# A three-stage fp32 block on one core: staged first transfers, a third load by rows of 128, and the last convolution taps ahead of a weight split

## The reference, cut to what matters

```python
h = rms_norm(x, mix_pre_g[0])                      # 256 x 2048
z = h @ ab_w_in                                    # 2048 x 3072 of weights
u_pool, v, gate = z[:, :1024], z[:, 1024:2048], z[:, 2048:]
c = causal_depthwise_conv(v * sigmoid(gate), conv_w) + conv_b    # 31 taps, 1024 channels
y_conv = silu(layer_norm(c, ln_g, ln_b))
m = concat(multiscale_pool(u_pool), y_conv) @ ab_w_out
x = x + rms_norm(m, mix_post_g[0])
...                                                # two MLPs, a short convolution, attention, gating
```

## Time and profile before

| what | value |
|---|---|
| median of 3 runs | 2687.98 us |
| the profiled execution's own time | 2690.7 us |
| its span | 2689.0 us |
| TensorE busy | 2679.8 us of the span (100%) |
| VectorE busy | 1872.4 us (70%) |
| ScalarE busy | 1292.8 us (48%) |
| GpSimd busy | 278.2 us (10%) |
| read from HBM | 511.47 MB, 191 GB/s over the span |

### The profile page before, as it was taken

How to read it: one execution, slowest core, us unless ns; L and a number is a source line. 1 busy time by engine, 2 the same in 40 slices (tenths; PEclk the granted TensorE clock), 3 DMA queues, 4 the chain that set the end, 5 groups by cost and what they waited for, 6 DMA issues and landing times.

```text
span 2689.0 us, 31099 instructions
## 1 busy us (share of the span) xinstructions
PE 2679.8 (100%) x12001; PEld 2218.5 (83%) x12001; DVE 1872.4 (70%) x2495; ACT 1292.8 (48%) x1635; POOL 278.2 (10%) x263
## 2 busy tenths in 40 slices
PE   9999999999999999999999999999999999999999
PEld 7888888888888888888888888888888888888887
DVE  6878777666866767776677676667767757765564
ACT  6765544434444454444544444344445446544452
POOL 4851100000000010000110000000011001000000
PEclk9999999999999999999999999999999999999999
DMA  7545665555555556555555555555555645455554
GB/s 248 183 169 180 215 211 183 184 202 188 193 192 195 194 183 213 193 197 194 187 188 204 203 188 186 190 188 203 188 188 179 211 173 182 169 200 194 188 188 156
DMA packets 267972, 515.58 MB, mean 192 GB/s; under 512 B 8450, under 2 KB 27956, under 8 KB 267316
## 3 DMA queue, kind: packets, MB, share of 16 engines
q1 hardware_dynamic: 267556, 513.34, 55.4%
q10 hardware_dynamic: 272, 0.26, 0.0%
HBM read 511.47 MB, written 2.10 MB: 191 GB/s over the span
## 4 chain that ended last, share of the span: by engine, by line
PE 98%; DMA 1%; DVE 1%; ACT 0%; issue 0%; SPq 0%
PE bank L786 32%; PE bank L788 32%; PE bank L787 32%; PE bank L837 1%; DMA x_res<-in_x 0%; DMA w_raw<-in_ab_w_in 0%; PE bank L854 0%; PE bank L1027 0%; DVE w_lo L765 0%; PE bank L988 0%; PE bank L1041 0%; PE bank L1014 0%; DVE w_lo L755 0%; DVE bank L1783 0%; PE bank L1048 0%
## 5 line engine op out<-in xcount | busy, mean ns | idle before, releaser
L765 DVE TENSOR_TENSOR w_lo<-w_raw,w_hi 128x1024 fp32r<-128x1024 f32 x952 | 1183.1, 1265 | 493.5 <-ACT w_hi L747 487.8
L747 ACT ACTIVATE w_hi<-w_raw 128x1024 fp32r<-128x1024 f32 x956 | 974.7, 1056 | 589.9 <-PE bank L788 432.9
L786 PE MATMUL bank<-w_hi,A_lo 128*128 128x512 f32 x2432 | 952.5, 392 | 2.3 <-DVE A_lo L1468 0.8
L788 PE MATMUL bank<-w_hi,A_hi 128*128 128x512 f32 x2432 | 947.2, 389 | 0.0
L787 PE MATMUL bank<-w_lo,A_hi 128*128 128x512 f32 x2432 | 946.7, 389 | 0.0
L786 PE MATMUL bank<-w_hi,B_lo 128*128 128x512 f32 x1408 | 548.7, 390 | 0.0
L788 PE MATMUL bank<-w_hi,B_hi 128*128 128x512 f32 x1408 | 547.9, 389 | 0.0
L787 PE MATMUL bank<-w_lo,B_hi 128*128 128x512 f32 x1408 | 547.8, 389 | 0.0
L786 PEld LDWEIGHTS bank<-w_hi,A_lo 128*128 128x128 f32 x2432 | 456.6, 188 | 98.4 <-DVE w_lo L765 2.3
L788 PEld LDWEIGHTS bank<-w_hi,A_hi 128*128 128x128 f32 x2432 | 456.4, 188 | 95.8
L787 PEld LDWEIGHTS bank<-w_lo,A_hi 128*128 128x128 f32 x2432 | 456.7, 188 | 93.2
(11 more groups left out here) (178 smaller groups left out, 975.7 us busy)
## 6 DMA issues: line engine op xcount, KB each, us to landing
w_raw<-in_ffn_w SPq DMA_DIRECT2D x256, 1024.0 KB, 5.1
w_raw<-in_w_in SPq DMA_DIRECT2D x88, 1024.0 KB, 4.9
w_raw<-in_sc_w_in SPq DMA_DIRECT2D x48, 1024.0 KB, 5.1
w_raw<-in_ab_w_out SPq DMA_DIRECT2D x16, 1024.0 KB, 5.0
w_raw<-in_sc_w_out SPq DMA_DIRECT2D x16, 1024.0 KB, 5.1
w_raw<-in_w_out SPq DMA_DIRECT2D x16, 1024.0 KB, 5.3
w_raw<-in_ab_w_in SPq DMA_DIRECT2D x28, 512.0 KB, 4.6
w_raw<-in_ab_w_in SPq DMA_DIRECT2D x8, 1024.0 KB, 5.1
```

The lines of the kernel that those rows point to most:

```text
L747: e.activation(w_hi[:, s % SPLIT_SLOTS, :], raw_step(s), ACT.Copy).then_inc(hi_made, 1)
L765: e.tensor_tensor(w_lo[:, slot, :], raw_step(s), w_hi[:, slot, :].bitcast(F32), ALU.subtract).then_inc(lo_made, 1)
L786: e.matmul(ps, lo[:, kt, tok], wh, start=first, stop=False)
L788: ins = e.matmul(ps, hi[:, kt, tok], wh, start=False, stop=last)
```

## The change

The first transfers are issued in stages: in front of most of them SyncE now waits until an earlier one has landed. Load 2 is brought by four `load_rows` of 256 KB in place of one `load_weights` with two pieces of 512 KB, and `BEGIN` covers 6 steps, so that steps 4 and 5 are split by 128-row parts too. ScalarE and VectorE make the halves of group 1 of `x` in two parts, with step 2's weights split between them and step 3's behind. VectorE does step 57's taps right behind step 56's, which puts them ahead of the low half of step 60.

```diff
-        BEGIN = 2 * STEPS_PER_LOAD
-        rows_loaded = [semaphore(f"rows_loaded{i}") for i in range(2 * GK)]
+        BEGIN = RAW_SLOTS * STEPS_PER_LOAD
+        rows_loaded = [semaphore(f"rows_loaded{i}") for i in range(RAW_SLOTS * GK)]
...
-            before = LOADED[n - RAW_SLOTS] if n >= RAW_SLOTS + 2 else 0
+            before = LOADED[n - RAW_SLOTS] if n >= 2 * RAW_SLOTS else 0
...
             load_rows(0, 0)
             load_rows(0, 1)
             e.dma_start(x[:, :, CH // 2:CH], x_dram[:, :, CH // 2:CH]).then_inc(x_loaded[0], 16)
+            e.wait_ge(x_begun, 16)
             load_rows(0, 2)
+            e.wait_ge(rows_loaded[0], 16)
             load_rows(0, 3)
+            e.wait_ge(rows_loaded[1], 16)
             load_x(1)
-            for k in range(GK):
-                load_rows(1, k)
+            e.wait_ge(x_loaded[0], 16)
+            load_rows(1, 0)
+            e.wait_ge(rows_loaded[2], 16)
+            load_rows(1, 1)
+            e.wait_ge(rows_loaded[3], 16)
+            load_rows(1, 2)
+            load_rows(1, 3)
+            e.wait_ge(x_loaded[1], 16)
             load_x(2)
-            load_weights(2)
+            e.wait_ge(rows_loaded[4], 16)
+            load_rows(2, 0)
+            e.wait_ge(rows_loaded[5], 16)
+            load_rows(2, 1)
+            e.wait_ge(rows_loaded[6], 16)
+            load_rows(2, 2)
+            load_rows(2, 3)
+            e.wait_ge(x_loaded[2], 16)
             load_x(3)
...
-            hi_x(0, 1)
+            for h in two:
+                hi_half(0, 1, h)
+                split_to(e, split_hi, at, STEPS_PER_LOAD + h)
...
-            lo_x(0, 1)
+            for h in two:
+                lo_half(0, 1, h)
+                split_to(e, split_lo, at, STEPS_PER_LOAD + h)
...
-                for tap in taps_at(DVE_TAPS, POS[c, i], DVE_TAP_TO):
-                    dve_tap(e, *tap)
+                s = POS[c, i]
+                for step in (s, s + 1) if s == DVE_TAP_TO - 2 else (s,) if s < DVE_TAP_TO - 1 else ():
+                    for tap in taps_at(DVE_TAPS, step, DVE_TAP_TO):
+                        dve_tap(e, *tap)
```

More of the change, by code:

```diff
@@ L1084, in hi_scaled, with hi_half @@
                 e.activation(halves[buf][0][:, kt + 1, :], view[:, 1, :], ACT.Copy, scale=gains[1]).then_inc(hi_cast(*key), 1)
+            def hi_half(p, g, h):
+                kt = GK * g + 2 * h
+                hi_scaled("A", kt, [par_col(PRE_COL[p], kt + k) for k in two], "pre", p, g, h)
             def hi_x(p, g):
                 for h in two:
-                    kt = GK * g + 2 * h
-                    hi_scaled("A", kt, [par_col(PRE_COL[p], kt + k) for k in two], "pre", p, g, h)
+                    hi_half(p, g, h)
             def hi_tile(p, g, tt):
@@ L1470, in lo_scaled, with lo_half @@
                 ins.then_inc(lo_cast(*key), 1)
+            def lo_half(p, g, h):
+                kt = GK * g + 2 * h
+                lo_scaled("A", kt, [par_col(PRE_COL[p], kt + k) for k in two], "pre", p, g, h)
             def lo_x(p, g):
                 for h in two:
-                    kt = GK * g + 2 * h
-                    lo_scaled("A", kt, [par_col(PRE_COL[p], kt + k) for k in two], "pre", p, g, h)
+                    lo_half(p, g, h)
             def lo_part(p, g, tt, h):
```

## The result

The changed kernel is slower: 2695.7 us, the median of 9 runs (2693.97 to 2697.49), against 2687.98 us before (9 runs, 2687.55 to 2688.68). The ratio is 1.0028, 95% interval 1.0018 to 1.0038. I had forecast 2687.6 us, no change. A loss of more than 0.2% had a chance of 0.05, 0.04 of it in the last of my rivals, the slow stages at 2696.4 us. The time lies outside the range of 2684.6 to 2690.6 us.

A forecast was written before the change was run, and what follows sets the result against it. TensorE bounds the kernel, busy 2679.8 of 2689.0 us. Start 0 and taps -0.4 us, put to the median of 2687.98 us, gave 2687.6 us; range 2684.6 to 2690.6 us, about 0.85.

The forecast's parts named there:

- the slow stages: Rival, start: waits leave transfer engines empty, 512 KB still takes 8.8 us, step 6 at 40.7 us: 2696.4 us; chance 0.04.
- The bound: TensorE's waits: only some 3.5 us, 0.13% of the time, could be won.
- The path to load 3: SyncE's queue: groups 1 to 3 in stages of 4.4 us, small transfers, then load 3, landing at 27.5 us.
- my bad end of 31.5 us: Load 3's latest believed landing, with 5.5 us per 512 KB transfer; step 6 then at 35.9 us.
- Load 3 lands later: Rival, start: 5 us a stage and 8 us for load 3, step 6 at 34.2 us: 2689.9 us; chance 0.15.
- The estimate of 3.2 us for 512 KB: Staged transfers: the skill page's figures give 3.2 us for 512 KB; step 6 would start at 29.5 us.
- The same difference put to it gives 2687.98 - 0.4: Final sum: the median lies 2.7 us below the profiled execution; the same difference gives 2687.6 us.
- my forecast of 31.9 us: Start: load 3 lands at 27.5 us and step 6 starts at 31.9 us, as in the profile before; sum 0.
- The clock: Rival, wait before step 6: clock falls to 1.2 GHz, costing 1.9 us: 2689.5 us; chance 0.16.
- Gain 0.33 to 0.5 us: Taps near 190.8 us: moved early, they remove TensorE's wait of 0.33 us; 0.4 us taken.
- Load 2 by rows and the order of group 1: Start: VectorE's extra 0.8 us is covered, step 4 can begin 0.45 us sooner; the order adds no instruction.

The follow-up runs named there:

- experiment 5: The kernel before, unchanged, profiled once more: own time 2687.83 us, span 2686.1 us.
- experiment 1: The changed kernel without its eleven waits on SyncE's queue: 2687.88 us, ratio 1.0002 to the kernel before.
- experiment 6: The kernel before with the early taps alone: 2688.08 us, ratio 1.0000.
- experiments 9: The changed kernel itself, timed and profiled a second time: 2694.49 us, ratio 1.0024 to the kernel before.
- experiment 2: The kernel before with the eleven waits alone, load 2 still two pieces of 512 KB: 2694.01 us, ratio 1.0020.
- Experiment 3: The changed kernel with 40 more transposes of the identity on TensorE ahead of step 6: 2693.73 us, ratio 1.0022 to the kernel before.
- Experiment 12: The changed kernel without waits, small transfers on GpSimd's queue, and step 62's high half ahead of the layer norm: 2686.25 us, ratio 0.9994 to the kernel before.
- Version 8: The changed kernel without its waits and with the 14 small transfers on GpSimd's queue: 2687.05 us, ratio 0.9996 to the kernel before.
- version 11: The kernel before with only the 14 small transfers moved to GpSimd's queue: 2687.59 us, ratio 0.9998.
- 10: The changed kernel with all eleven waits and the 14 small transfers on GpSimd's queue: 2688.77 us, ratio 1.0001 to the kernel before.
- 4: The changed kernel, all waits kept, with load 3 issued ahead of the 14 small transfers: 2688.44 us, ratio 1.0002 to the kernel before.

## Why the prediction was wrong

**The bound: right in kind, too large.** I put what could be won at 3.5 us. 1.73 us of that and some of the 0.8 us at step 6 belong to the first profiled execution; in that of experiment 5 it is 1.3 us. No version gained more than 1.6 us, and that one moves the small transfers too. Taking away the small waits ahead of step 6 was worth nothing as long as load 3 set that step: in experiment 1 step 4's wait is gone, and TensorE stands 0.86 us before step 6, which starts 0.2 us sooner than in experiment 5.

**The path to load 3: the right mechanism, sized too small at each link.** Between stages I took 4.4 us for 512 KB; it was 5.26 and 4.87 us, 1.3 us for the two less 0.3 us by which the first began sooner. The small transfers and the issue of group 3 took 6.5 us in place of 5.9 (15.73 to 22.27), one of them 1.22 us for an issue of 0.42. Load 3 took 7.7 us (22.27 to 29.95) in place of 6.9. Together load 3 landed at 29.95 us in place of 27.5, inside my bad end of 31.5 us, and step 6 came 2.4 us later than forecast. The rival "Load 3 lands later", with 5 us a stage and 8 us for load 3, has step 6 at 34.2 us; 34.35 us were measured. It was right on the path, and its 2689.9 us fell short for the two reasons that follow. The last rival, the slow stages, has 2696.4 us, near the measured time, but that is chance: it wants 8.8 us for a 512 KB transfer and step 6 at 40.7 us. The estimate of 3.2 us for 512 KB that the prediction made from the Trainium skill (DMA: Bandwidth & Descriptors, Anatomy of one DMA) is too low for every stage: in the executions with all the waits and transfers on SyncE the two took between 4.1 and 6.2 us each. The section gives its fit for transfers that GpSimd issues, and these are SyncE's.

**"The same difference put to it gives 2687.98 - 0.4": the step that failed first.** I had a row that the profiled execution took 2.7 us more than the median of the runs. I carried this as an offset of the profile and measured the start against that execution's 31.93 us. Experiment 5 shows that it was the start itself that was slow: usually step 6 begins at 29.26 us. Against this even my forecast of 31.9 us was a loss of 2.6 us. The real loss of step 6 is 34.35 - 29.26 = 5.1 us. That the 29.26 us are usual rests on one profile whose own time, 2687.83 us, is close to the median; in the profile of experiment 6, which has the same start, step 6 began at 30.02 us with a span 0.8 us longer.

**The clock: right mechanism, put at nothing in the sum.** The sum of the forecast has no term for it. I gave 0.16 to a fall of the clock beside a step 6 at 31.9 us, and only some 0.01 to the clock on top of a late load 3. But the two are one case: the later step 6, the longer TensorE stands still. Idle for 6.1, 5.25 and 3.58 us it fell in each of three executions; idle for 2.29 and 1.73 us it did not. From 34.35 us to 40.4 us the changed kernel started 14 matmuls, which take 14 x 0.23 = 3.2 us at the full pace: 2.9 us lost, where the rival had 1.9. In the same way 1.6 us are lost in the profiles of experiments 9 and 2. With the later start of step 6 that gives 8.0, 6.8 and 5.8 us; the spans are 8.0, 6.8 and 5.7 us over that of experiment 5. Experiment 3 kept the clock up without touching the waits, and there the late start alone gives the 6.0 us of the span. The Trainium skill (TensorE: Matmul & The Clock Gate, Part 1) has the array's clock halved when the engine has been idle; the granted clock of 0.50 from within the idle stretch on agrees.

**The taps: the step "Gain 0.33 to 0.5 us" fell.** The wait went and came back 14 us later as 0.26 us (0.64 us from start to start in experiment 6, against 0.23 us usually). I had asked only whether step 60's low half was late, and not what TensorE would next be too early for. Experiment 12 shows the cause by taking it away. It holds for the version of 8; on the kernel before alone it was not tried.

**Load 2 by rows and the order of group 1: right.** They cost nothing that shows, and step 4's wait of 0.67 us (0.70 in experiment 5) is gone in every version that has them. Version 8, which has them, is 1.0 us under the kernel before beside it; version 11, which has not, 0.6 us.

**The sum as it should have been:** 5.1 us for step 6, 2.9 us for the clock, 0 for the taps: 8.0 us. The spans differ by 2694.1 - 2686.1 = 8.0 us and the medians by 7.7 us (6.3 us in the second series). Against the forecast the miss is 2.6 us for the start taken from an execution that began late, 2.4 us for the links sized too small, 2.9 us for the clock and 0.4 us for the taps.

**What the first waits are for.** Held against the execution that I had read, they do what they seem to: the second half of group 0 lands at 6.24 us in place of 8.8, group 1 at 10.83 in place of 12.58. Held against that of experiment 5, where the two land at 6.95 and 10.16 us, they win 0.7 us for the first and lose 0.7 us for the second, and the landing of group 1 decides. The greater price is paid by what stands behind them. Removing the small transfers from the queue (10) leaves 0.6 us of a loss of 6.3 us; removing the waits (1) leaves none.

**Left open.** Why some executions have a slower start is not settled. In the one profiled, the second half of group 0 took 6.6 us to land and group 1 8.8 us. A transfer lands in 16 parts, and its trace shows that 15 parts of these two had landed by 6.65 and 10.53 us and the last at 8.81 and 12.58 us; in experiment 5 the last part came 0.2 and 0.4 us behind the rest. What held that part was not tried. The runs of the kernel before at 2689 us or more are 10 of 56 on the two chips of experiments 1 to 4 and 9 to 11, and none of 42 on those of experiments 5 to 8 and 12, so the chip may have a share in it.

## What to carry to other kernels

A wait in front of a transfer delays everything behind it in the same queue, so count the way to the last urgent transfer: rounds of issue to landing, plus every small issue between. Give small transfers a queue of their own before staging the large ones. When a profiled execution takes longer than the median of the runs, find where in it the excess lies before using its start as the base of a sum. When a wait is taken away from the bounding engine, ask which of its next waits has less margin than the gain. And a late start can cost twice, once for the idle time and once for the clock behind it.

## What the runs showed of the hardware that I had not expected

- The granted clock was down at 0.50 after 3.58 us of idle TensorE in one execution (experiment 2). It stayed low for 10.2 us in one execution of the changed kernel, TensorE at work in the last 6.1 of them, and for 3.4 us in another, at work in nearly all of them.
- The full pace at the very start comes at different times too: the same eight transposes took 1.04 us from 5.42 us in one execution of the kernel before and 1.91 us from 5.59 us in the other (experiment 5). The granted clock reads 1.00 in both stretches, so only the durations tell.
- Issuing a small transfer took some 0.5 us on GpSimd's queue (0.7 us for the first) and mostly 0.25 to 0.55 us on SyncE's, where the last of them took 1.2 to 1.6 us in the executions of the result and of experiments 2 and 9. The 14 of them took GpSimd from 2.82 to 10.18 us. Its convolution bands ended at 28.4 us in place of 19.6, and no wait of TensorE names them.
- An unchanged program's first 12 us differ between executions: group 1 took 8.8 us from issue to landing in one and 6.4 us in another.
